# First token tables of a mixture of experts from counts of logits, and two prefetched weight parts issued at other points

## What is computed

```python
def reference(x, ...):
    xn = rms_norm(x, norm_mix[l])
    x = x + token_mixer(xn, w_in[l], ...)
    hn = rms_norm(x, norm_ffn[l])
    x = x + hier_moe(hn, router_group_w[l], ...)
    return rms_norm(x, norm_final)

def hier_moe(x, w_rg, b_rg, w_re, b_re, w_gate, w_up, w_down):
    g_logits = xt @ w_rg + b_rg                      # 4 groups
    g_idx = argmax(g_logits); g_w = softmax(g_logits)[g_idx]
    e_sel = (xt @ w_re + b_re).reshape(t, 4, 8)[:, g_idx]
    top_v, top_i = lax.top_k(e_sel, 2)               # 2 of the group's 8 experts
    top_w = softmax(top_v) * g_w
    # 32 experts, each silu(x @ gate) * (x @ up) @ down, 1024 -> 256 -> 1024
```

## Time and profile before

| what | us |
|---|---|
| median of 3 runs | 603.55 (603.31 to 603.91) |
| span of the profiled execution | 601.3 |
| PE busy | 576.4 (96%) |
| DVE busy | 262.7 (44%) |
| ACT busy | 216.4 (36%) |
| GpSimd busy | 60.5 (10%) |

### The profile page before, as it was taken

How to read it: one execution, slowest core, us unless ns; L and a number is a source line. 1 busy time by engine, 2 the same in 40 slices (tenths; PEclk the granted TensorE clock), 3 DMA queues, 4 the chain that set the end, 5 groups by cost and what they waited for, 6 DMA issues and landing times.

```text
span 601.3 us, 8737 instructions
## 1 busy us (share of the span) xinstructions
PE 576.4 (96%) x3437; PEld 436.4 (73%) x3440; DVE 262.7 (44%) x610; ACT 216.4 (36%) x440; POOL 60.5 (10%) x104
## 2 busy tenths in 40 slices
PE   7999999999999999999999998999999999896896
PEld 4978989888788888888888875666666666553552
DVE  4645677645445766533472386112111211113255
ACT  6644666555786522422252251111111111111114
POOL 3110000001000001100000022021212121112001
PEclk9999999999999999999999999999999999989999
DMA  8365130712231222197789667999999999999995
GB/s 309 80 209 175 59 112 4 289 61 71 71 105 42 65 70 71 36 335 277 289 317 414 257 237 309 384 419 423 423 422 425 423 425 420 424 426 424 423 421 217
DMA packets 59292, 155.78 MB, mean 259 GB/s; under 512 B 8285, under 2 KB 38389, under 8 KB 47601
## 3 DMA queue, kind: packets, MB, share of 16 engines
q1 hardware_dynamic: 54512, 145.74, 63.3%
q0 software_dynamic: 4720, 9.45, 4.1%
q10 hardware_dynamic: 16, 0.00, 0.0%
HBM read 147.31 MB, written 15.75 MB: 271 GB/s over the span
## 4 chain that ended last, share of the span: by engine, by line
PE 85%; DMA 7%; DVE 4%; SPq 1%; ACT 1%; issue 1%; POOL 1%; DVEq 0%; POOLq 0%; ACTq 0%
PE mid_rows L813 17%; PE last_rows L813 16%; PE bank L1271 15%; PE bank L813 7%; PE mid_rows L1291 7%; PE bank L806 6%; DMA slot2b<-expert_w_up 5%; PE bank L1345 2%; PE last_rows L871 2%; PE mid_rows L948 2%; SPq L555 1%; PE mid_rows L1364 1%; PE bank L1371 1%; DMA w<-w_in 1%; PE mid_rows L871 1%
## 5 line engine op out<-in xcount | busy, mean ns | idle before, releaser
L1271 PE MATMUL bank<-slots,xgT 128*64 128x256 f32 x544 | 74.7, 384 | 3.9 <-DMA slot2b<-expert_w_up 2.2
L1944 DVE TENSOR_TENSOR w_low<-w,w_high 128x1024 fp32r<-128x1024 f32 x32 | 39.2, 1225 | 78.6 <-ACT w_high L1548 78.6
L1271 PEld LDWEIGHTS bank<-slots,xgT 128*64 128x64 f32 x544 | 49.4, 138 | 22.9 <-issue 4.4
L1548 ACT ACTIVATE w_high<-w 128x1024 fp32r<-128x1024 f32 x32 | 33.7, 1054 | 48.6 <-PE last_rows L813 48.6
L2370 DVE TENSOR_SCALAR y<-mid_rows,slot_weights 128x512 f32<-128x512 f32 x14 | 10.5, 750 | 86.1 <-PE mid_rows L1291 86.1
L1733 ACT ACTIVATE y<-mid_rows,slot_weights 128x512 f32<-128x512 f32 x14 | 9.6, 687 | 81.3 <-PE mid_rows L1291 59.6
L1271 PE MATMUL bank<-slot2b,xgT 128*64 128x256 f32 x208 | 34.6, 390 | 0.0
L1291 PE MATMUL mid_rows<-slots,hT 128*64 128x512 f32 x112 | 29.1, 594 | 1.3 <-issue 1.3
L1727 ACT ACTIVATE h_silu<-bank 128x256 f32<-128x256 f32 x14 | 5.4, 384 | 68.5 <-PE bank L1271 68.5
L813 PE MATMUL mid_rows<-x_high,w_high 128*128 128x512 f32 x72 | 28.6, 398 | 0.0
L813 PE MATMUL mid_rows<-x_high,w_low 128*128 128x512 f32 x72 | 28.1, 390 | 0.0
(11 more groups left out here) (445 smaller groups left out, 1397.3 us busy)
## 6 DMA issues: line engine op xcount, KB each, us to landing
slots<-expert_w_up SPq DMA_DIRECT2D x18, 1024.0 KB, 24.2
slots<-expert_w_gate SPq DMA_DIRECT2D x17, 1024.0 KB, 12.4
slots<-expert_w_down SPq DMA_DIRECT2D x15, 1024.0 KB, 23.8
slot2b<-expert_w_gate SPq DMA_DIRECT2D x9, 1024.0 KB, 17.4
w<-w_in SPq DMA_DIRECT2D x16, 512.0 KB, 3.6
slot2b<-expert_w_up SPq DMA_DIRECT2D x8, 1024.0 KB, 27.9
slot2a<-expert_w_down SPq DMA_DIRECT2D x6, 1024.0 KB, 21.4
w<-w_in SPq DMA_DIRECT2D x7, 840.0 KB, 4.6
```

Of the source, the lines that this page charges most:

```text
L1271: ins = mm(bank[2][e * SLOTS:(e + 1) * SLOTS, m * FE:(m + 1) * FE], xgT[:, c, e * SLOTS:(e + 1) * SLOTS], weights(own, m, e, c * FE, (c + ...
L1548: A(wh2[:, u % 2, :], raw2[:, u % 2, :], ACT.Copy).then_inc(s["hi_done"], 1)
L1944: V.tensor_tensor(wl2[:, u % 2, :], raw2[:, u % 2, :], wh2[:, u % 2, :].bitcast(F32), ALU.subtract).then_inc(s["lo_done"], 1)
```

## The change

DVE computes the first two pairs' tables (experts 0 to 3, all in group 0) by another way and earlier. For each of these four experts it counts the logits of the group that beat this one: greater, or equal and at a smaller index. A token has chosen the expert if group 0 has its best group logit and fewer than 1.5 logits beat the expert's. PE ranks these choices by itself, DVE forms `first_place`, one `hot` matrix for each of the pairs 0 and 1, and PE makes a table column for each; DVE turns it to integers in one instruction, as the token numbers are halved beforehand. The second choices of the first half of the tokens are put off behind the second half's logits. The general tables follow: the products of all 16 pairs are run between the first pair's gate and up products (`all_tokens`), and their integers come behind the first pair's other work on DVE.

On the other engines: SP issues part 16 without a wait for the first two stores, part 20 behind the issue of the first gather (`pool_step`) instead of behind the stores alone, and part 22 behind the landing of the first gather as before, and also behind `fast_in`. GpSimd sets the buffer to zero when two stores have landed, and waits for the other two behind it (`hn_late`). ACT makes all four copies of the first turned rows. `keep_busy` products go from 37 to 24 in this stretch. Two semaphores are merged into others (`norm_in`, `v_out`).

```diff
+        FAST = 4
+        beats = place_at(fast_at, "beats", NT * FAST * NE)...
-        first_slots = place_at(0, "first_slots", P)[:, :]
+        first_slots = K["triF"].rearrange("p (j n) -> p j n", j=2)
...
 SP
-            sp.wait_ge(s["hn_out"], 16 * (ZERO_PIECES + 2))
             for t in range(2, NT):
                 load_part(16 + t - 2)
                 store_rows(t)
...
-            sp.wait_ge(s["hn_out"], 16 * (ZERO_PIECES + NT))
+            sp.wait_ge(s["pool_step"], 1)
+            sp.wait_ge(s["hn_late"], 32)
             sp.wait_ge(s["hT_done"], 2 * NT)
             load_part(20)
             sp.wait_ge(s["x2_done"], 2 * NT)
+            sp.wait_ge(s["fast_in"], 4)
             sp.wait_ge(s["gathered0"], 16)
             load_part(22)
...
 GpSimd
-            pool.wait_ge(s["hn_out"], 16 * (ZERO_PIECES + NT))
-            pool.wait_ge(s["hT_done"], 2 * NT)
+            pool.wait_ge(s["hn_out"], 16 * (ZERO_PIECES + 2))
+            pool.wait_ge(s["hT_done"], NT)
             nc.gpsimd.memset(xg_in, 0.0).then_inc(s["zeroed"], 1)
             pool.wait_ge(s["zeroed"], 8)
+            pool.wait_ge(s["hn_late"], 32)
...
 PE
-            keep_busy(14)
+            keep_busy(4)
+            pe.wait_ge(s["fast_in"], 2)
+            for t in range(NT):
+                for u in range(t + 1):
+                    ins = mm(bank[4][:, t * FAST:(t + 1) * FAST], (beforeb if u == t else onesb)[:, :], first_sel[:, u, :],
+                             start=(u == 0), stop=(u == t), skip_group_check=True)
+            ins.then_inc(s["first_done"], 1)
+            keep_busy(4)
+            for j in range(2):
+                pe.wait_ge(s["fast_in"], j + 3)
+                for t in range(NT):
+                    ins = mm(bank[3][:, TABLE][:, 2 * j:2 * j + 2], hot[:, NT * j + t, :], by_pair[:, t, 0:2], ...)
+                ins.then_inc(s["first_done"], 1)
+                keep_busy((3, 8)[j])
             pe.wait_ge(s["selb_done"], 1)
...
             keep_busy(5)
-            (table products of pair 0, keep_busy(8), table products of all pairs, keep_busy(10))
+            def all_tokens(): (table products of all pairs)
...
 turn_first
+                    if c == 4:
+                        pe.wait_ge(s["fast_in"], 5)
...
             turn_first()
             gate_or_up(0, 0, *weights_of(0), halved=True)
+            all_tokens()
...
 ACT, first_x
+                for q_, (b_, at) in enumerate(((0, 0), (1, 0), (3, 0), (4, 2 * P))):
+                    act.wait_ge(s[("first_done", "xt_done")[q_ % 2]], (4, 1, 5, 2)[q_])
+                    A(xgT[:, 2 * q_:2 * q_ + 2, :], bank[b_]..., ACT.Copy).then_inc(s["fxT_out"], 1)
...
 DVE
+            def first_experts(ts, g_):
+                e_ = step(V.tensor_tensor(beats[:, ts], e_lg[:, ts, 0, :]..., bc(e_lg[:, ts, 0, 0:FAST], NE), ALU.is_gt))
+                after(g_)
+                step(V.tensor_tensor(first_group[:, ts], lg[:, ts, 0], gmax[:, ts], ALU.is_equal))
+                after(e_)
+                for x_ in range(1, FAST):
+                    e_ = step(V.tensor_tensor(beats[:, ts, x_, 0:x_], e_lg[:, ts, 0, 0:x_], bc(e_lg[:, ts, 0, x_], x_), ALU.is_ge))
+                after(e_)
+                after(step(V.tensor_reduce(beaten_by[:, ts], beats[:, ts], AX, ALU.add)))
+                V.scalar_tensor_tensor(out=first_sel[:, ts], in0=beaten_by[:, ts], scalar=1.5, in1=bc(first_group[:, ts], FAST),
+                                       op0=ALU.is_lt, op1=ALU.mult).then_inc(s["fast_in"], 1)
+            def first_hot(j): (hot[:, 4j to 4j + 3] = first_slots equal first_place)
+            def first_table(j):
+                dve.wait_ge(s["first_done"], j + 2)
+                V.tensor_scalar(gtab[:, j:j + 1], bank[3][:, TABLE][:, 2 * j:2 * j + 1], NOWHERE / 2.0, None, ALU.add
+                                ).then_inc(s["gcolm_done"], 1)
...
             g_, e_ = maxima_of(lo)
+            first_experts(lo, g_)
...
-            e_, d_ = at_second(lo, e_)
-            e_, _ = second_keyed(lo, e_, d_)
-            l_ = second_key(lo, e_)
             router_out(2, 4, 6)
             dve.wait_ge(s["rl_out"], 2)
-            g_, e_ = maxima_of(hi)
+            g_ = step(V.tensor_reduce(gmax[:, hi], g_lg[:, hi], AX, ALU.max))
+            first_experts(hi, g_)
+            e_ = step(V.tensor_reduce(v1[:, hi], e_lg[:, hi], AX, ALU.max))
+            l_, d_ = at_second(lo, l_)
             g_, e_ = at_maximum(hi, g_, e_)
+            l_, _ = second_keyed(lo, l_, d_)
+            dve.wait_ge(s["first_done"], 1)
+            after(step(V.scalar_tensor_tensor(out=first_place, in0=bank[4]..., scalar=1.0, in1=first_sel, op0=ALU.add, op1=ALU.mult)))
+            first_hot(0)
+            l_ = second_key(lo, l_)
             g_, e_ = keyed(hi, g_, e_)
             g_, e_ = best_key(hi, g_, e_)
+            first_table(0)
+            first_hot(1)
             g_, e_ = first_choice(hi, g_, e_)
...
             e_ = second_maximum(hi, g_, e_)
+            first_table(1)
```

More of the change, by code:

```diff
@@ L259, in hybrid_encoder @@
         group_exp = place_at(SMALL + 960, "group_exp", NT * NG)[:, :].rearrange("p (t i) -> p t i", t=NT)
-        assert 3 * NT * EXPERTS + 6 * NT * NE <= 768
+        FAST = 4
+        fast_at = SMALL + 3 * NT * EXPERTS + 6 * NT * NE
+        beats = place_at(fast_at, "beats", NT * FAST * NE)[:, :].rearrange("p (t x i) -> p t x i", t=NT, x=FAST)
+        beaten_by, first_place = (v3(place_at(fast_at + NT * FAST * (NE + i_), n_, NT * FAST), FAST)
+                                  for i_, n_ in enumerate(("beaten_by", "first_place")))
+        first_group = place_at(fast_at + NT * FAST * (NE + 2), "first_group", NT)
+        first_sel = v3(place_at(fast_at + NT * FAST * (NE + 2) + NT, "first_sel", NT * FAST, BF16), FAST)
+        assert fast_at + NT * FAST * (NE + 3) + NT <= SMALL + 768
         by_weight = lg[:].rearrange("p t n -> p (t n)")[:, 0:2 * NT * PAIRS].rearrange("p (k j) -> p k j", k=2 * NT)
@@ L605, in store_rows @@
                 sp.wait_ge(s["hn_done"], t + 1)
-                sp.dma_start(hn_dram[t * P:(t + 1) * P, :], hn_st[:, t, :]).then_inc(s["hn_out"], 16)
+                sp.dma_start(hn_dram[t * P:(t + 1) * P, :], hn_st[:, t, :]).then_inc(s["hn_out" if t < 2 else "hn_late"], 16)
             sp.wait_ge(s["lo_done"], LOWS + len(units))
@@ L1193, in _ @@
                start=False, stop=False, skip_group_check=True)
-            keep_busy(14)
+            keep_busy(4)
[9 more added lines that the diff above has]
+                for t in range(NT):
+                    ins = mm(bank[3][:, TABLE][:, 2 * j:2 * j + 2], hot[:, NT * j + t, :], by_pair[:, t, 0:2], start=(t == 0),
+                             stop=(t == NT - 1), skip_group_check=True)
+                ins.then_inc(s["first_done"], 1)
+                keep_busy((3, 8)[j])
             pe.wait_ge(s["selb_done"], 1)
@@ L1205, in _, with all_tokens @@
             keep_busy(5)
[L1207 to L1219, removed]
+            def all_tokens():
+                for k in range(2 * NT):
+                    pe.wait_ge(s["hot_done"], k + 1)
+                    ins_ = mm(bank[3][:, TABLE][:, 0:PAIRS], hot[:, k, :], by_pair[:, k, :], start=(k == 0),
+                              stop=(k == 2 * NT - 1), skip_group_check=True)
+                ins_.then_inc(s["first_done"], 1)
             def slot_weights():
                 pe.wait_ge(s["hTs_done"], 1)
-                pe.wait_ge(s["hot_done"], 4 * NT + 1)
+                pe.wait_ge(s["hot_done"], 2 * NT + 1)
                 for k in range(2 * NT):
@@ L2124, in _ @@
                 split_low2(u)
+            V.tensor_scalar(first_slots[:, 0, :].rearrange("p (x e l) -> p x e l", l=4, e=8),
+                            K["iota"][:, 0:SLOTS].rearrange("p (x l e) -> p x e l", l=4, e=8), 1.0, None, ALU.add)
+            for i in range(2):
+                V.tensor_scalar(first_slots[:, 1, :].rearrange("p (x e i l) -> p i x e l", l=4, i=2, e=4)[:, i],
+                                K["iota"][:, 0:SLOTS].rearrange("p (x l e i) -> p i x e l", l=4, i=2, e=4)[:, 1 - i], 1.0, None, ALU.add)
+            V.tensor_scalar(by_pair[:, 0:NT, 0:2], K["tokval"][:, 0:NT].unsqueeze(2).to_broadcast([P, NT, 2]), 0.5, None, ALU.mult)
             def residual(t):
@@ L2276, in _ @@
             V.tensor_tensor(selb[:], sel[:, 0], sel[:, 1], ALU.add).then_inc(s["selb_done"], 1)
[L2277 to L2281, removed]
+            l_ = step(V.tensor_copy(dealt.rearrange("p (x e l) -> p x e l", l=4, e=8),
+                                    K["iota"].rearrange("p (x l e) -> p x e l", l=4, e=8)))
             dve.wait_ge(s["rank_done"], 1)
@@ L2286, in _ @@
             link(V.tensor_reduce(place[:].rearrange("p (k t) -> p k t", k=2), sel[:], AX, ALU.add))
[L2288 to L2291, removed]
+            dve.wait_ge(s["cnt_done"], 1)
+            V.tensor_copy(cnt[:, 0:EXPERTS], bank[4][0:1, P:P + EXPERTS]).then_inc(s["fast_in"], 1)
```

68 lines of the change are left out of this document (32 added, 36 removed).

## The result

| | us | ratio to before, 95% interval |
|---|---|---|
| before | 603.67 (603.31 to 603.91, 4 runs) | |
| changed | 607.05 (606.38 to 608.76, 4 runs) | 1.0062 (1.0045 to 1.0079) |

The change makes the kernel 3.4 us slower. The forecast was 3.0 us faster, with a range from 599.5 to 603.9. The profiled execution of the changed kernel has a span of 605.4 us against 601.3; it was already 0.5 us behind when the output projection ended, a difference in which the change has no part.

The account below looks back on a forecast made before the run. Bound by weight bytes at 424 GB/s, so an earlier first gather helps: 3.7 us earlier, less 0.45 for the gather and 0.25 for the queue, gives 3.0 off 603.55, or 600.5 us; range 599.5 to 603.9.

Parts of the forecast that it names:

- What bounds the kernel: From some 386 us on, the end depends on weight bytes still to come at 424 GB/s, not on PE time.
- the 326 GB/s in 378 to 382: Weights' rate around the first gather in the kernel before, read as a queue that is not full.
- The table: On DVE, first token column ready at 363.4 instead of 367.09, 3.7 us earlier; gather issued at 364.3.
- The counts copied out: DVE's fast_in 5, which PE waits for: forecast at 368.6, while PE needs it at about 369.6.
- the eight table products: all_tokens on PE between the first pair's gate and up products: adds 0.95 us, mostly hidden by queued weights.
- ACT's four copies: ACT copies all turned rows, 0.38 us each, just ahead of PE: costs nothing, or 0.4 us at most.
- The stores: Part 16 issued up to 2.3 us earlier; fourth store lands at 362.8 instead of 364.7, hidden behind the table.
- Part 20 and the gather itself: Part 20 issued near 365.4 behind the gather's issue, costing nothing; first gather takes 4.9 us, landing at 369.2.
- Rival B: Part 20 beside the first gather gives it 8.1 us: landing at 372.4, no gain, time 603.9; chance 0.15.
- Rival D, the clock: Less fill lets PE idle; first pair at half clock takes 7.06 us more, time 606.8; chance 0.06.
- The other page cited: DMA engines taking turns at packet boundaries would land the first gather at 368.75, time 600.1; not the rule followed.
- the part behind the up product: First weight part released by the first pair's up product: issued at 378.5 instead of 380.77.

Follow-up runs that it names:

- e5: Changed kernel with part 20 issued when DVE has summed the choices (wait on selb_done instead of pool_step); 600.27 us, ratio 0.9945.
- e1: Changed kernel with 15 more fill products on PE in front of the first turned rows; 602.85 us, ratio 0.9987.
- e4: Kernel before with part 20 issued behind the first gather's landing; 605.20 us, ratio 1.0026.
- e10: Kernel before with part 20 issued when its last table is ready, behind the first gather's issue; 604.76 us, ratio 1.0008.
- e8: Changed kernel with part 20 issued when the second token column is ready (gcolm_done instead of pool_step); 606.81 us, ratio 1.0047.
- e3: Kernel before without the 10 fill products directly in front of the first turned rows; 605.94 us, ratio 1.0028.
- e7: Changed kernel with part 20 behind the first gather's landing and part 16 again waiting for the first two stores; 603.58 us, ratio 0.9990.
- e2: Changed kernel with part 20 issued behind the first gather's landing instead of behind its issue; 602.25 us, ratio 0.9962.

## Why the prediction was wrong

**What bounds the kernel** was right. The weights' queue is full at 423 GB/s from 402 on in both kernels, and the time follows the bytes moved by then: from 350 to 402 the changed kernel moved 16.6 MB, the kernel before 18.1 and e5 19.3, and the 2.6 MB between the first and the last are 6.2 us at 423 GB/s, of 6.8 us measured. One reading was not right: the 326 GB/s in 378 to 382 are no gap, as the DMA share there is 1.01.

**The table** was right. It came at 363.65 against 363.4 forecast, in an execution that ran 0.5 us late; the gather's instruction at 364.60 against 364.3. The counts copied out came at 368.36 against 368.6, the eight table products took 0.99 against 0.95, and ACT's four copies left no wait in e1's chain.

**The stores** were mis-sized: 8.87 us instead of the 8.5 taken (362.8), a tie with the table, without effect.

**Part 20 and the gather itself** is the step that failed. The prediction had part 20 issued "near 365.4", behind the gather's instruction, and the gather at 4.9 us. It was issued at 364.41, ahead of the gather, since the semaphore that it waits for goes up before the gather's work is in the queues, and the gather took 7.58: its first packets were held until 369.0. I had read 4.45 us in the trace of before as what a gather takes beside one part in flight. That part had been issued 3.3 us ahead and was ending as the gather's packets began; e4 and e10 have 3.4 us without it. With the table 3.4 us earlier and part 20 where it was, the gather met the whole of it. I had also taken for first packets that the weights held back. They were not held: in e4 they move in the same half microsecond with the queue empty. Why they were held in the changed kernel, for the same 4.4 us as in e8, stays open. (Part 20 belongs to the up product of the fourth pair, not to a down product as the prediction has it; nothing rests on that.)

Rival B had this number, with 8.1 us and a landing at 372.4 (372.2 measured), at a chance of 0.15. Its reason, that part 20 runs beside the gather, is not enough: in e5 it does, behind the gather's first packets, and the gather takes 4.2 us. Its price of 603.9 left out what comes next on PE, and does not come out of its own terms, which give 603.7 to 604.4.

**Rival D, the clock,** was the second half, at 0.06. I weighed it against idle stretches of 0.3 to 1 us, taken from a gather that lands at 369.2. With the landing of B there are 3.63 us of idle time, more than the 1.54 us in front of the fall in the earlier trace rows. The two are one case, not two: B brings D about. D's price of 606.8 is near the measured 607.05 by luck: it took the gather for on time and the first pair for 7.06 us longer, where PE lost 2.75 us behind a late gather. e1 puts the clock at 4.2 us and e5 puts the place of part 20 at 6.8 us, in which the clock's share is contained, so the rest is some 2.6 us. The page "TensorE: Matmul & The Clock Gate" of the Trainium skill, in "Part 1: The HAM clock gate", has the clock follow PE's recent activity, and the traces of the changed kernel, e3, e7 and e8 agree.

The other page cited did not help the gather here. "DMA: Bandwidth & Descriptors" of the Trainium skill, in "Queues, rings and completion order", has the engines take turns between queues at packet boundaries. Once the gather's packets moved, that fits the traces: 22 of them beside 16 of the weights in the half microsecond from 369.0, and 80.0% beside 26.1% in e5. It does not show in the changed kernel and e8 before that, where no packet of the gather moved for 4.4 us, against 1.9 us in e2, e4 and e5. What held the first ones was not tried.

With part 20 really behind the gather, the kernel takes 600.27 us (e5); the forecast was 600.5. The sum was that of another kernel: in e5 the gather lands at 368.7 (369.2 forecast) and the part behind the up product is issued at 378.1 (378.5). But e5 issues part 20 at 366.7; the 365.4 of the prediction, 0.8 us behind the gather's recorded start and so inside its instruction, was not run.

## What to carry to other kernels

A semaphore that counts "behind the indirect DMA" in GpSimd's program can go up before the DMA is in the queues. If a bulk load must not get ahead of a small urgent transfer, tie it to something later than that. Here 1.0 us behind the end of GpSimd's instruction was enough (e5); nearer was not tried. Before a table or an index is made earlier, ask what will be queued at the new time: the duration of the transfer at the old time does not say. Fill products belong to the wait that they cover: if a change moves that wait, they must move with it. Here the clock alone cost 4 us, in a change that was to win 3.

## What the runs showed of the hardware that I had not expected

- A part of 1 MB issued 0.2 us ahead of the recorded start of a gather's instruction, or 0.6 us behind it, delays a gather of some 0.2 MB by 3.4 to 4.1 us (7.6 and 8.25 against 4.2); issued 2.2 us behind the start, it delays it by 0.3 at most (4.2 against 3.9).
- The gather's first packets moved 1.9 us behind the recorded start of its instruction in the kernel before, e2, e4, e5 and e10, whether the weights' queue was empty (e4) or not. In the changed kernel and e8 it was 4.4 us.
- After 1.9 us of idle time in e7, 2.4 in e3 and 3.6 in the changed kernel the clock was at 0.50. In the changed kernel a product of 3.60 us took 5.54, and PE lost 2.75 us in all, which came with 4.2 us of kernel time. Its weights' rate was 383 GB/s from 386 to 402, against 420 in e1, with the DMA engines busy for 0.99 and 1.01 of it. What the lower rate comes from is not shown; e3 has 424 GB/s there, after the same fall of the clock.
